# Recurrence readout with statistics in the token domain, a hand-over normalised tile by tile, and an experts' loop written out

## The chip, the cores and the metric

The kernel runs on one core of one Trainium2 chip. The metric is device time in microseconds (us) of one execution. Every time below comes from the runs of the kernel before or from its one profiled execution.

## The reference, cut to what matters

The program computes one forward pass in float32: two hybrid attention layers over 528 tokens (512 and 16 meta tokens), a final RMS norm, and then a second model over the 512 tokens and 256 context tokens: neighbourhood attention, a mixture of experts, an RWKV-7 recurrence in both directions, and a second mixture of experts. Three places are touched.

```python
# end of the first model, whose result is the second model's x
return rms_norm(h, final_g)[:, N_META:]

# readout of the recurrence; y is (token, head, 64)
mu = jnp.mean(y, axis=-1, keepdims=True)
var = jnp.mean(jnp.square(y - mu), axis=-1, keepdims=True)
yn = ((y - mu) * lax.rsqrt(var + RW_GN_EPS)).reshape(B, T, -1) * ln_g + ln_b
bonus = jnp.sum(jnp.sum(r[None] * kt * r_k, axis=-1, keepdims=True), axis=0) * v
return ((yn + bonus.reshape(B, T, -1)) * g) @ w_o
```

The mixture of experts has 16 experts with a 1024-wide hidden layer. Each takes 64 latent tokens and, in the first mixture, 32 context tokens too; its three weight matrices are 12 MiB.

## The kernel before, in words

The program is a row of stages. Each stage (`stage`, L48) is a block with one instruction stream per engine and ends with a barrier of all engines, so a stage takes as long as its slowest engine. Weights come through a ring of three slots of 2 MB (`load_chunk`, L73), which SyncE (its queue is called SP) fills when the stage's TensorE work has freed a slot.

**Hand-over** (`second_start`, L1064). It stands between the two models. SP issues `gain` (L1074), 17 small resident tensors (L2939), four rows of gates broadcast to 128 partitions (L1077), waits until the gates have landed (L1078), and only then issues the two tiles of context tokens (L1080). ScalarE sums the squares of four tiles (L1090) and takes one root over all four (L1093). VectorE inverts it (L1100), waits for `gain`, scales the four tiles (L1103), works on the modulation columns (L1108, L1113) and, last, waits for everything loaded (L1116). The first stages after it are `norm_turn` and `neighbour_project`, whose SP waits for TensorE's products before it loads a chunk.

**Experts** (`experts`, L1643), once after each attention layer. TensorE, ScalarE and VectorE each run a hardware loop of four passes (`Fori`) over a body of four experts. For each expert TensorE multiplies six half-matrix chunks (helper at L1750: 24 matmuls per chunk with context tokens, 8 without), places one-hot rows (L1760), turns the hidden rows (L1773) and the next expert's tokens (L1766). SP's and GpSimd's streams are already written out.

**Readout** (`rwkv_readout`, L2728). Y and V lie with 64 tokens times two heads on the partitions, and eight chunks of (pair, 64 features) behind each other. TensorE turns Y and V of one pair of heads at a time into features on partitions, with 16 matmuls against a 64-wide identity (L2764). It subtracts the mean by a product with a centring matrix (L2780), makes the gate (L2781), and sums the squares over each head by a product with ones (L2789). ScalarE copies (L2804), squares (L2813), adds the bias (L2817) and takes the root (L2821) of 128x512 tiles. VectorE inverts the 128x512 root (L2828) and does three more passes (L2830, L2833, L2836). GpSimd multiplies V by the bonus (L2755). The eight pairs follow each other with two buffers of each kind. After the stage, `hold` (L2839) issues the loads of the output weights, and `add_projection` (L999, matmuls at L1021) multiplies by them.

## Time and profile before

| | us |
|---|---|
| median of 3 runs | 3743.45 (3739.27 to 3749.13) |
| the profiled execution | 3760.89 |
| its span in the trace | 3759.1 |
| TensorE matmul busy | 3249.7 (86%) |
| VectorE busy | 1548.5 (41%) |
| ScalarE busy | 825.0 (22%) |
| GpSimd busy | 263.6 (7%) |
| mean granted clock of TensorE, share of full | 0.934 |

The profiled execution is one run with its own disturbances; 1.8 us lie outside its span. Matmul busy time is modelled from issue to end, and since matmuls are pipelined a busy TensorE says little by itself. What ends a wait is read from the name behind the arrow. A float32 matmul is recorded as two.

### The profile page before, as it was taken

How to read it: one execution, taken by the hardware profiler on the slowest of the kernel's cores; microseconds unless marked ns; L12 is line 12 of the kernel's file. 1: busy time of each engine (PE TensorE's matmuls, PEld its weight loads, DVE VectorE, ACT ScalarE, POOL GpSimd, SP SyncE). 2: the span in 40 equal slices, each digit the busy share in tenths (PEclk: the TensorE clock that was granted, in tenths of full speed). 3: DMA queues.
4: the chain of work that ended last, by engine and by line, in shares of the span. 5: the costliest groups of instructions: out<-in, count | busy, mean ns of one | idle time of the engine just before them, and what ended most of it. 6: DMA issues, size and time to landing. Idle time of an engine off the chain costs nothing. (4 is left out here: it accounts for less than half of the span.)

```text
span 3759.1 us, 73325 instructions
## 1 busy us (share of the span) xinstructions
PE 3249.7 (86%) x32052; PEld 1860.4 (49%) x32052; DVE 1548.5 (41%) x3486; ACT 825.0 (22%) x1777; POOL 263.6 (7%) x253
## 2 busy tenths in 40 slices
PE   7997999989699999699999969977888877677877
PEld 5845558555344564343343434557777753222222
DVE  4665435654212572422121244157777763311111
ACT  2104210142111570000000010046555530000000
POOL 0000000000000110000000000001222210000000
PEclk9998899988899999799999989979999998799999
DMA  6663046700221102599999921100000003699998
GB/s 176 170 184 108 23 96 165 210 24 29 86 67 48 32 25 90 216 379 337 345 367 338 347 67 67 40 25 4 4 4 4 4 30 122 254 401 399 403 400 347
DMA packets 147234, 605.36 MB, mean 161 GB/s; under 512 B 17264, under 2 KB 20144, under 8 KB 129904
## 3 DMA queue, kind: packets, MB, share of 16 engines
q1 hardware_dynamic: 140592, 579.19, 42.5%
q0 software_dynamic: 6336, 21.63, 2.5%
q8 instruction: 249, 4.08, 0.5%
q14 instruction: 57, 0.47, 0.0%
HBM read 576.00 MB, written 31.07 MB: 161 GB/s over the span
## 5 line engine op out<-in xcount | busy, mean ns | idle before, releaser
L1750 PE MATMUL psum<-ring,big 128*64 128x512 f32 (+1 forms) x6144 | 918.3, 506 | 117.9 <-DMA ring<-moe_w 99.8
L1750 PEld LDWEIGHTS psum<-ring,big 128*64 128x64 f32 (+1 forms) x6144 | 305.3, 126 | 711.0 <-issue 492.3
L1888 DVE TENSOR_TENSOR big<-big,psum 128x512 f32<-128x512 f32 (+1 forms) x48 | 27.3, 596 | 650.8 <-PE psum L1750 650.8
L391 PE MATMUL psum<-h_uT,ring 128*128 128x264 f32 x1280 | 290.5, 387 | 0.0
L520 DVE SCALAR_TENSOR_TENSOR h_O<-h_O,cond_silu 128x512 f32<-128x512 f32 x336 | 226.7, 744 | 102.7 <-DMA h_O<-ada_w 102.7
L391 PEld LDWEIGHTS psum<-h_uT,ring 128*128 128x128 f32 x1280 | 242.0, 190 | 46.5 <-issue 5.8
L1235 PE MATMUL psum<-ring,big 128*128 128x512 f32 x576 | 252.4, 598 | 1.7 <-PEq L55 1.7
L2328 PE MATMUL psum<-ring,gates 64*64 64x128 f32 (+1 forms) x5120 | 170.6, 257 | 81.8 <-ACT ring L2511 74.6
L2328 PEld LDWEIGHTS psum<-ring,gates 64*64 64x64 f32 x5120 | 134.3, 135 | 97.5 <-DVE ring L2669 83.5
L1900 DVE SCALAR_TENSOR_TENSOR big<-psum,big,gates 64x512 f32<-64x512 f32 (+1 forms) x128 | 78.8, 615 | 247.2 <-PE psum L1750 245.8
L1235 PEld LDWEIGHTS psum<-ring,big 128*128 128x128 f32 x576 | 109.5, 192 | 135.4 <-issue 135.4
L411 PE MATMUL psum<-ring,h_uT 128*128 128x512 f32 x384 | 170.0, 600 | 0.0
L1827 ACT ACTIVATE big<-psum 128x512 f32<-128x512 f32 (+1 forms) x48 | 23.5, 524 | 594.8 <-PE psum L1750 594.8
L1021 PE MATMUL psum<-ring,big 128*128 128x512 f32 x320 | 139.6, 598 | 16.6 <-DMA ring<-rw_w_o 15.5
L2669 DVE TENSOR_TENSOR ring<-ring,psum 64x256 f32<-64x256 f32 x288 | 120.9, 420 | 3.9
L411 PEld LDWEIGHTS psum<-ring,h_uT 128*128 128x128 f32 x384 | 72.6, 192 | 91.2 <-issue 91.1
L2511 ACT ACTIVATE gates<-psum 128x512 f32<-128x512 f32 x120 | 71.4, 595 | 183.7 <-PE psum L2328 183.5
L2056 PE MATMUL psum<-big,ring 128*128 128x512 f32 (+1 forms) x336 | 110.4, 491 | 0.0
L1718 POOL DMA_INDIRECT big<-rows,index x34 | 40.4, 1188 | 964.4 <-DVE big L1852 964.4
L1021 PEld LDWEIGHTS psum<-ring,big 128*128 128x128 f32 x320 | 61.3, 192 | 94.3 <-issue 78.0
L2328 PE MATMUL psum<-big,ring 64*64 64x64 f32 (+1 forms) x2816 | 105.5, 240 | 0.0
L1295 DVE TENSOR_REDUCE stat<-sq 128x8 f32<-128x512 f32 x24 | 16.5, 686 | 211.5 <-ACT sq L1274 211.5
(344 smaller groups left out, 4534.7 us busy)
## 6 DMA issues: line engine op xcount, KB each, us to landing
ring<-moe_w SPq DMA_DIRECT2D x192, 2048.0 KB, 10.6
h_O<-ada_w SPq DMA_DIRECT2D x192, 256.0 KB, 3.0
ring<-w_in SPq DMA_DIRECT2D x16, 2048.0 KB, 15.2
ring<-na_w_qkv SPq DMA_DIRECT2D x6, 2048.0 KB, 8.0
ring<-w_out SPq DMA_DIRECT2D x4, 2048.0 KB, 8.7
bias_rows<-na_table SPq DMA_DIRECT2D x16, 480.0 KB, 16.1
ring<-bias_rows SPq DMA_DIRECT2D x16, 360.0 KB, 3.0
rows<-big SPq DMA_DIRECT2D x10, 512.0 KB, 4.4
```

Source lines behind the costliest of these rows:

```text
L391: last = nc.tensor.matmul(bank(k, pair_bank(q) + h, NH), w[:, a, f * P:(f + 1) * P], uT[:, a, halves[h]], start=a == 0, stop=a == KD - 1)
L411: last = nc.tensor.matmul(bank(k, b), uT[:, a, t * P:(t + 1) * P], w[:, a, :], **st)
L520: nc.vector.scalar_tensor_tensor(into, ada(u), by, into, ALU.mult, ALU.add).then_inc(s.acc, 1)
L1021: last = nc.tensor.matmul(bank(k, j % BANKS)[0:rows, :], srcT[:, a, t * P:t * P + rows], w[:, a, :], start=a == 0, stop=a == KD - 1)
L1235: last = nc.tensor.matmul(bank(k, j % FIRST_BANKS), hT[:, a, t * P:(t + 1) * P], w[:, a, :], start=a == 0, stop=a == KD - 1)
L1718: nc.gpsimd.indirect_dma_start(xg[0:M, e % 2, :], None, k.rows[:, :], bass.IndirectOffsetOnAxis(ap=index[0:M, e % ROUND:e % ROUND + 1], ax ...
L1750: last = nc.tensor.matmul(bank(k, b, r.width)[q * r.n:(q + 1) * r.n, :], rowsT[:, half * HALF_K + n, r.first:r.first + r.n], w[:, n, q * r ...
L1900: last = nc.vector.scalar_tensor_tensor(y[r.first:r.first + r.n, x % 2, cols], bank(k, r.downs, r.width)[mine, :], gate[mine, x, 2 * r.at ...
L2056: last = nc.tensor.matmul(bank(k, j % BANKS, n), w[:, a, at:at + P], xs[m][:, a, first:first + n], **st)
L2328: last = nc.tensor.matmul(bank(k, b, width, at + p % QUAD * width)[to:to + CH, :], lhs(lo, p), rhs(lo, p), start=start and n == 0, stop=st ...
L2511: copy = lambda out, got: nc.scalar.activation(out, got, ACT.Copy)
L2669: last = tt(new[there], old[here], got[there, 1, :, :], ALU.add)
```

## The change

Three parts, each in a stage of its own.

1. In `second_start` the context tiles are issued before the resident tensors, and the gates move into the SP stream of `neighbour_project`, whose end now waits for them. ScalarE takes a root after each tile, VectorE does the modulation columns first, and then inverts and scales tile by tile.
2. In `experts` TensorE's loop is a Python loop: the four passes are written out, with constants for the registers. The loops of ScalarE and VectorE stay.
3. `rwkv_readout` is written anew. Mean, centring and variance are taken on Y before it is turned: VectorE reduces each chunk over 64 features (mean), centres it with a broadcast, reduces ScalarE's squares, and inverts 128x8 roots; GpSimd multiplies by the inverse. Meanwhile TensorE turns V and makes the gates of all pairs, with four banks for each, and ScalarE moves both to SBUF. When all eight chunks are normalised, TensorE turns Y pair by pair, VectorE adds the scaled Y to the V term, and the last product with the gate alternates between GpSimd (even pairs) and VectorE (odd pairs).

```diff
@@ second_start
         def _(sp):
             if norm:
                 sp.dma_start(gain[:, :], k.d["final_g"].partition_broadcast(P)).then_inc(s.gain_here, 16)
-            total = load_resident(k, sp, tiles, s.here)
-            for g in range(4):
-                sp.dma_start(k.gates[:, g, :], k.mod_rows[0, g % 2, (2, 5)[g // 2] * D:((2, 5)[g // 2] + 1) * D].partition_broadcast(P)).then_inc(k.gates_here, 16)
-            sp.wait_ge(k.gates_here, 64)
             for t in range(CT):
                 sp.dma_start(k.X[:, LT + t, :], k.d["ctx_2"][0, t * P:(t + 1) * P, :]).then_inc(s.here, 16)
+            total = load_resident(k, sp, tiles, s.here)
             sp.wait_ge(s.here, total + 16 * CT)
...
+            for t in range(LT if norm else 0):
+                dve.wait_ge(s.rooted, t + 1)
+                nc.vector.reciprocal(stat[:, 2, t:t + 1], stat[:, 1, t:t + 1]).then_inc(s.inverted, 1)
+                dve.wait_ge(s.inverted, t + 1)
+                if t == 0:
+                    dve.wait_ge(s.gain_here, 16)
+                nc.vector.scalar_tensor_tensor(k.X[:, t, :], k.X[:, t, :], stat[:, 2, t:t + 1], gain[:, :],
+                                               ALU.mult, ALU.mult).then_inc(s.normed, 1)
             dve.wait_ge(s.here, 16 * (len(tiles) + CT))
@@ neighbour_project, SP
+            for g in range(4):
+                sp.dma_start(k.gates[:, g, :], k.mod_rows[0, g % 2, (2, 5)[g // 2] * D:((2, 5)[g // 2] + 1) * D].partition_broadcast(P)).then_inc(k.gates_here, 16)
             for n in range(4):
                 sp.wait_ge(s.product, n_tiles * (n + 1))
...
             sp.wait_ge(s.between, 32)
+            sp.wait_ge(k.gates_here, 64)
@@ experts, TensorE
-            with pe.Fori(0, EXPERTS // ROUND) as it:
+            for it in range(EXPERTS // ROUND):
@@ rwkv_readout, GpSimd
+            def scale(c):
+                pool.wait_ge(s.inverted, c + 1)
+                nc.gpsimd.tensor_tensor(Y[:, c, :, :], Y[:, c, :, :], over(2, c), ALU.mult).then_inc(s.normed, 1)
+
+            pool.wait_ge(s.sorted, 4)
+            for p in range(QUAD):
+                shade(p)
+            for p in range(QUAD, PAIRS):
+                scale(p - QUAD)
+                shade(p)
+            for c in range(PAIRS - QUAD, n_chunk):
+                scale(c)
+            for p in range(0, PAIRS, 2):
+                pool.wait_ge(s.closed, p + 1)
+                nc.gpsimd.tensor_tensor(mixT[:, p, :], term(p), gate(p), ALU.mult)
@@ rwkv_readout, TensorE
             for p in range(PAIRS):
...
                 pe.wait_ge(s.shaded, p + 1)
+                if p >= QUAD:
+                    pe.wait_ge(s.v_out, p - QUAD + 1)
+                turned(V, p % QUAD, p, p >= QUAD).then_inc(s.v_turned, 1)
...
+            pe.wait_ge(s.normed, n_chunk)
+            for p in range(PAIRS):
+                if p < QUAD:
+                    pe.wait_ge(s.v_out, p + QUAD + 1)
+                else:
+                    pe.wait_ge(s.gate_out, p + 1)
+                turned(Y, p, p, False).then_inc(s.y_turned, 1)
@@ rwkv_readout, ScalarE
+            for n in range(n_chunk):
+                act.wait_ge(s.centred, n + 1)
+                if n >= 2:
+                    act.wait_ge(s.spread, n - 1)
+                nc.scalar.activation(square(n), Y[:, n, :, :], ACT.Square).then_inc(s.squared, 1)
+                if n:
+                    root(n - 1)
+                act.wait_ge(s.v_turned, n + 1)
+                nc.scalar.activation(term(n), bank(k, n % QUAD), ACT.Identity, bias=k.ln_cols[:, 1, n:n + 1]).then_inc(s.v_out, 1)
+                act.wait_ge(s.gate_made, n + 1)
+                nc.scalar.activation(gate(n), bank(k, QUAD + n % QUAD), ACT.Copy).then_inc(s.gate_out, 1)
+            root(n_chunk - 1)
@@ rwkv_readout, VectorE
+            def mean(c):
+                nc.vector.tensor_reduce(stat[:, 0, c, :], Y[:, c, :, :], AX.X, ALU.add).then_inc(s.summed, 1)
+                dve.wait_ge(s.summed, c + 1)
+                nc.vector.scalar_tensor_tensor(Y[:, c, :, :], over(0, c), -1.0 / CH, Y[:, c, :, :], ALU.mult, ALU.add).then_inc(s.centred, 1)
...
+            for c in range(n_chunk):
+                mean(c)
+                if c >= 2:
+                    invert(c - 2)
+                if c >= 1:
+                    spread(c - 1)
...
             for p in range(PAIRS):
...
+                dve.wait_ge(s.y_turned, p + 1)
                 dve.wait_ge(s.v_out, p + 1)
+                nc.vector.scalar_tensor_tensor(term(p), bank(k, p), k.ln_cols[:, 0, p:p + 1], term(p), ALU.mult, ALU.add).then_inc(s.closed, 1)
+                if p % 2:
+                    dve.wait_ge(s.closed, p + 1)
+                    dve.wait_ge(s.gate_out, p + 1)
+                    nc.vector.tensor_tensor(mixT[:, p, :], term(p), gate(p), ALU.mult)
```

VectorE in the readout. Before, each pair of heads has these four full-width passes:

```order
L2825 SCALAR_TENSOR_TENSOR big<-head_ones_sb,ident_sb 128x128
L2828 RECIPROCAL big<-big 128x512
L2830 TENSOR_TENSOR big<-psum,big 128x512
L2833 SCALAR_TENSOR_TENSOR big<-big,ln_cols_sb 128x512
L2836 TENSOR_TENSOR big<-big,psum 128x512
```

Now each chunk has two reductions, one centring pass and a reciprocal of 128x8, and the pairs come at the end:

```order
L2840 TENSOR_REDUCE big<-big 128x8
L2834 TENSOR_REDUCE big<-big 128x8
L2836 SCALAR_TENSOR_TENSOR big<-big 128x512
L2844 RECIPROCAL big<-big 128x8
...
L2858 SCALAR_TENSOR_TENSOR big<-psum,ln_cols_sb,big 128x512 x2
L2862 TENSOR_TENSOR big<-big 128x512
```

The reciprocal went from 512 columns to 8, and the statistics of all chunks now stand ahead of the first turned Y.

TensorE at the end of the first mixture's loop body, before (L1750 the products, L1785 the loop):

```order
L1766 MATMUL psum<-ident_sb,big 128x96 x8
L1750 MATMUL psum<-ring,big 64x512 x8
L1750 MATMUL psum<-ring,big 32x256 x16
L1743 REGISTER_ALU
L1750 MATMUL psum<-ring,big 64x512 x8
L1750 MATMUL psum<-ring,big 32x256 x16
L1785 REGISTER_ALU
L1785 COMPARE_AND_BRANCH
```

Now, between any two experts:

```order
L1760 MATMUL psum<-big 128x2 x6
L1773 MATMUL psum<-ident_sb,big 128x128 x6
L1766 MATMUL psum<-ident_sb,big 128x96 x8
L1750 MATMUL psum<-ring,big 64x512 x8
L1750 MATMUL psum<-ring,big 32x256 x16
```

The branch is gone after every fourth expert; the matmuls are the same.

SP's queue at the hand-over, before (end of the stage) and now (its beginning, then its end with the next SP stage):

```order
L2939 DMA head_ones_sb<-head_ones 128x128
L1077 DMA gates<-mod_rows 128x1024 x4
L1080 DMA X<-ctx 128x1024 [waits gates_here]
L1080 DMA X<-ctx 128x1024
```

```order
L1075 DMA gain<-final_g 128x1024
L1077 DMA X<-ctx 128x1024 x2
L2966 DMA na_q_cols_sb<-na_q_cols 128x1
...
L2966 DMA head_ones_sb<-head_ones 128x128
L52 UNCONDITIONAL_BRANCH [waits here_1]
L1196 UNCONDITIONAL_BRANCH [waits barrier_Pool_Activation_PE_DVE_SP_release]
L1199 DMA gates<-mod_rows 128x1024 x4
```

The wait on the gates is gone from between the two groups of loads, and the gates stand behind the barrier.

## Rows read from the trace of the kernel before

**Rows 1.** Waits between 950 and 1000 us: waiter, releaser, total, times, longest.

```profile
SPq L1080 <- DMA gates<-mod_rows: 7.5, 1, 7.5
...
DVE na_q_cols_sb L1116 <- DMA X<-ctx: 9.0, 1, 9.0
```

**Rows 2.** Timeline of the hand-over: start, duration, engine, line, operation.

```profile
958.59 0.34 SPq L1074 DMA_DIRECT2D gain<-final_g  x1
...
966.49 5.25 DVE L1103 SCALAR_TENSOR_TENSOR X<-X,stat,gain 128x1024 f32<-128x1024 f32 x4 [2.74 <-DMA gain<-final_g]
...
981.60 0.15 DVE L1116 TENSOR_SCALAR na_q_cols_sb<-na_q_cols_sb 128x1 f32<-128x1 f32 x1 [9.00 <-DMA X<-ctx]
```

**Rows 3.** Timeline of TensorE in the first mixture of experts.

```profile
1615.62 32.76 PE L1750 MATMUL psum<-ring,big 128*64 128x512 f32 x288
...
1651.62 32.76 PE L1750 MATMUL psum<-ring,big 128*64 128x512 f32 x288
...
1702.69 23.56 PE L1750 MATMUL psum<-ring,big 128*64 128x512 f32 x192 [4.01 <-issue]
...
1802.31 34.46 PE L1750 MATMUL psum<-ring,big 128*64 128x512 f32 x288
...
1856.40 23.56 PE L1750 MATMUL psum<-ring,big 128*64 128x512 f32 x192 [3.69 <-issue]
...
2007.78 23.28 PE L1750 MATMUL psum<-ring,big 128*64 128x512 f32 x192 [5.42 <-issue]
```

**Rows 4.** Windows: length, busy PE, PEld, DVE, ACT, POOL; PEclk, DMA share, GB/s.

```profile
1590.00:1700.00 110.00, 108.39 (x954) 44.88 (x946) 25.93 (x68) 5.23 (x12) 7.97 (x6) 1.00 0.98 373
...
3300.00:3400.00 100.00, 78.39 (x358) 27.37 (x356) 13.96 (x33) 4.87 (x7) 8.05 (x6) 0.96 1.02 400
...
1699.00:1707.00 8.00, 4.31 (x12) 1.35 (x14) 3.18 (x6) 0.00 (x0) 1.43 (x1) 0.79 0.98 337
...
3055.00:3062.00 7.00, 5.08 (x66) 4.32 (x67) 0.29 (x1) 2.11 (x6) 5.87 (x6) 0.51 0.86 335
```

**Rows 5.** Timeline of TensorE in the second mixture, fourth and fifth expert.

```profile
3329.29 3.65 PE L1750 MATMUL psum<-ring,big 128*64 128x512 f32 x16 [2.77 <-DMA ring<-moe_w]
...
3361.91 9.09 PE L1750 MATMUL psum<-ring,big 128*64 128x512 f32 x32 [2.92 <-DMA ring<-moe_w]
```

**Rows 6.** Timeline of the readout and the projection after it.

```profile
3055.09 1.94 PE L2764 MATMUL psum<-eye_sb,big 64*64 64x64 f32 x32 [3.00 <-PEq L55]
...
3063.26 1.15 PE L2764 MATMUL psum<-eye_sb,big 64*64 64x64 f32 x32
...
3110.47 0.69 DVE L2836 TENSOR_TENSOR big<-big,psum 128x512 f32<-128x512 f32 x1
...
3119.91 56.93 PE L1021 MATMUL psum<-ring,big 128*128 128x512 f32 x128 [15.52 <-DMA ring<-rw_w_o]
```

**Rows 7.** Groups of the readout, 3054 to 3118 us: count, busy, mean ns, idle before.

```profile
L2828 DVE RECIPROCAL big<-big 128x512 f32<-128x512 f32 x8 | 26.8, 3346 | 11.7 <-ACT big L2821 11.7
...
L2755 POOL TENSOR_TENSOR big<-big,rw_bonus 128x512 f32<-128x512 f32 x8 | 8.2, 1058 | 2.1 <-ACT rw_bonus L2797 2.1
L2833 DVE SCALAR_TENSOR_TENSOR big<-big,ln_cols_sb 128x512 f32<-128x512 f32 x8 | 6.0, 752 | 0.3
...
L2804 ACT ACTIVATE big<-psum 128x512 f32<-128x512 f32 x8 | 4.8, 597 | 6.7 <-PE psum L2764 6.7
...
L2821 ACT ACT_TABLE_LOAD x1 | 1.3, 1283 | 0.0
```

**Rows 8.** Groups elsewhere with like operations; the last is one line's min, median, max.

```profile
L1295 DVE TENSOR_REDUCE stat<-sq 128x8 f32<-128x512 f32 x11 | 7.5, 686 | 56.6 <-ACT sq L1274 56.6
...
L1298 DVE RECIPROCAL stat<-stat 128x8 f32<-128x8 f32 x11 | 2.2, 203 | 3.0 <-ACT stat L1276 3.0
...
L2300 POOL TENSOR_TENSOR X<-ring,rw_R 128x512 f32<-128x512 f32 x16 | 28.2, 1765 | 72.8 <-DVE ring L2606 72.8
...
L2606 DVE SCALAR_TENSOR_TENSOR ring<-ring,big x24: 681/693/1012, 2496.4 to 2993.7; 128x512 f32<-128x512 f32 x24
```

More of the change, by code:

```diff
@@ L1066, in second_start @@
     nc = k.nc
-    with ExitStack() as mem, stage(k, "here scaled summed rooted step gain_here biased") as (block, s):
+    with ExitStack() as mem, stage(k, "here scaled summed rooted inverted normed gain_here biased") as (block, s):
         sb = lambda n, shape: mem.enter_context(nc.sbuf_tensor(f"{n}{k.stage_no}", shape, F32))
@@ L2725, in _, with rwkv_readout @@
             in_turn(slot)
-def rwkv_readout(k, Y, V, sums, tg, mixT, spare, g2):
+def rwkv_readout(k, Y, V, sums, tg, mixT, g2, stat, rest):
     nc = k.nc
@@ L2735, in rwkv_readout @@
     sums, bonus = sums
-    buf = lambda n: lambda p: spare[:, (2 * n + p % 2) * SEQ:(2 * n + p % 2 + 1) * SEQ]
-    yT, squares, root, term, scaled = (buf(n) for n in range(5))
-    centre = spare[:, 10 * SEQ:10 * SEQ + P]
-    Y_AT, MIDDLE_AT, GATE_AT = (lambda p: p % 2), (lambda p: 2 + p % 2), (lambda p: 4 + p % 2)
-    V_AT, SPREAD_AT = 6, 7
-    with stage(k, "g2_here restored sorted shaded centred y_turned v_turned middle gate_made spread "
-                  "y_out squared v_out rooted inverted normed shifted gated") as (block, s):
+    cut = lambda t, n: t[:, n * SEQ:(n + 1) * SEQ]
+    terms, low, high, squares = rest
+    term = lambda p: cut(terms, p)
+    gate = lambda p: cut(low if p < QUAD else high, p % QUAD)
+    square = lambda c: cut(squares, c % 2).rearrange("p (a i) -> p a i", i=CH)
+    stat = stat[:, 0:3 * n_chunk * PAIRS].rearrange("p (n c a) -> p n c a", n=3, c=n_chunk)
+    over = lambda n, c: stat[:, n, c, :].unsqueeze(2).to_broadcast([P, PAIRS, CH])
+    with stage(k, "g2_here restored sorted shaded v_turned v_out gate_made gate_out "
+                  "summed centred squared spread rooted inverted normed y_turned closed") as (block, s):
         @block.sync
@@ L2798, in _, with root @@
                                          ACT.Copy).then_inc(s.sorted, 1)
[L2800 to L2821 removed]
+            def root(c):
+                act.wait_ge(s.spread, c + 1)
+                nc.scalar.activation(stat[:, 1, c, :], stat[:, 1, c, :], ACT.Sqrt, bias=64e-5, scale=1.0 / CH).then_inc(s.rooted, 1)
@@ new lines, in spread, with invert @@
+            def spread(c):
+                dve.wait_ge(s.squared, c + 1)
+                nc.vector.tensor_reduce(stat[:, 1, c, :], square(c), AX.X, ALU.add).then_inc(s.spread, 1)
+            def invert(c):
+                dve.wait_ge(s.rooted, c + 1)
+                nc.vector.reciprocal(stat[:, 2, c, :], stat[:, 1, c, :]).then_inc(s.inverted, 1)
+            for c in range(n_chunk):
[4 more added lines that the diff above has]
+                    spread(c - 1)
@@ L2879, in rwkv_layer @@
         mixT = flat(A)[:, 0:KD * SEQ].rearrange("p (a b) -> p a b", a=KD)
-        rwkv_readout(k, Y, V, (sums, bonus), tg, mixT, flat(E), flat(A)[:, KD * SEQ:KD * SEQ + D])
+        rest = [flat(E)[:, 0:KD * SEQ], flat(C)[:, KD * SEQ:], left, flat(E)[:, KD * SEQ:KD * SEQ + D]]
+        rwkv_readout(k, Y, V, (sums, bonus), tg, mixT, flat(A)[:, KD * SEQ:KD * SEQ + D], flat(A)[:, KD * SEQ + D:], rest)
     hold(k)
```

76 lines of the change are left out of this document (12 added, 64 removed).

## The prediction

> **What bounds the kernel now.** Every stage ends at a barrier, so I read each of the three touched stages by itself, in the timeline and the waits. A microsecond taken off the last engine of a stage is taken off the whole time, unless the stage behind it is held by something that runs across the barrier.
>
> *Hand-over.* VectorE's last instruction starts at 981.60 [rows 2], after 9.0 us of waiting for the context tiles; those were issued after SP had waited 7.5 us for the gates, which nobody in this stage reads [rows 1]. VectorE's scaling had ended at 971.7 (966.49 + 5.25), with a few small operations behind it; those passes had waited for `gain` until 966.49 [rows 2]. A loading order bounds this stage.
>
> *First mixture of experts.* TensorE runs an expert without a gap: two begin at 1615.62 and 1651.62, 36.0 us apart, of which 32.76 are the products of six chunks [rows 3]. At the three loop ends it stands still for 4.01, 3.69 and 5.42 us, released by "issue", that is by nothing but its own sequencer [rows 3]. The four chunks behind each stop take 23.56, 23.56 and 23.28 us, where four sixths of 32.76 are 21.84. So the stage is bound by TensorE and its instruction stream. The weight stream is near it: 373 GB/s in a stretch without stops, where the second mixture shows that 400 can be had [rows 4].
>
> *Second mixture.* It is bound by that stream: DMA share 1.02 [rows 4], and TensorE waits for weights at the start of an expert whether a loop end lies before it (2.92 us) or not (2.77) [rows 5]. The two starts are 32.6 us apart, 12.6 MB at 386 GB/s.
>
> *Readout.* It runs from 3055.09 to 3111.16, 56.1 us [rows 6]. VectorE waits 11.7 us for the first root and is then busy to the end; of a pair's 5.5 us the full-width reciprocal is 3.35 [rows 7].
>
> **The change, part by part.**
>
> *Hand-over.* The gates (four issues) and the wait for them leave the stage. The context tiles are issued right behind `gain`. `gain` lands where it did, at about 966.4, and 1 MB behind it at 400 GB/s [rows 4] takes 2.6 us: 969. Two more issues put the last small load at about 968 and its landing at 970 to 971, est. VectorE then decides: from 966.5 four times 1.31 (5.25 / 4) [rows 2], a reciprocal of 0.2 at most [rows 8] and 0.05 of hand-off, 6.2: it ends at 972.9 instead of 981.75. The per-tile roots are ready before (`gain` is what is late) and cost nothing. **-8.8**; bounds -5.5 (small loads landing as late as the gates did) and -9.5. The gates now go out at the start of the projection stage, ahead of SP's waits for products: SP is free there, the ring is full, the queue empty; cost 0. Without that cover it would be the 7.5 us of rows 1.
>
> *Experts' loop written out.* First mixture: the three stops go, 4.01 + 3.69 + 5.42 = 13.1. Behind a stop the granted clock is at its lower level for a while (mean 0.79 of full over 8 us around the first, [rows 4]; the levels are 1.2 and 2.4 GHz), which made the four chunks 1.72, 1.72 and 1.44 longer, 4.9 in all. But the same loss of 1.7 shows in experts with no stop (34.46 against 32.76, [rows 3]), six times by my count of this trace, so it may come anyway. Some wait for weights may come too, since each stop let the loads catch up. I take **-16**: all stops and about half of the rest. Bounds 0 and -19. The register additions go too; they are too small to price. What new stall can the written-out stream bring? The loop body of four experts is already straight code of its kind, and in the 110 us up to about the first stop TensorE is busy 108.39 [rows 4]; I price the rest at 0. ScalarE's and VectorE's loops keep their branches; both have two or more chunks (11 us) before they are wanted. Second mixture: **0**, by rows 5.
>
> *Readout.* Removed: the centring and ones products, 8 x 3.35 of reciprocal, and the two buffers that tied TensorE, ScalarE and VectorE in one circle. Added, from like operations: per chunk two reductions at 0.69, a reciprocal of 128x8 at 0.20 [rows 8], a centring pass at 0.72 (between 0.69 and 0.75, [rows 7, 8]); on GpSimd one product at 1.05 [rows 7]. The path, in five pieces:
> - To the first inverse, 9.4 est: the bonus copies 1.0 and GpSimd's first product 1.05 with a wait of 0.4 before it, V turned 1.94 at the lower clock (granted clock 0.51 here, 1.2 GHz) [rows 4, 6], the gate product about as much, 1.7, two ScalarE passes at 0.60, the table load and root 1.5 [rows 7], the inverse 0.2, and 0.4 of hand-offs. Behind ScalarE's in-order waits for V and gate, VectorE's own 5 us of work is hidden.
> - Four periods with GpSimd's two products in each. GpSimd is slowed by VectorE when both read two SBUF tensors: 1765 ns for L2300, which starts 0.07 us after such a VectorE operation, against 1058 for one beside an idle VectorE; and once VectorE's L2606 took 1012 instead of 693 [rows 7, 8]. So I let them exclude each other. Inverse 0.20, GpSimd 1.05 + 1.05, centring 0.72, hand-offs 0.1: 3.1 x 4 = 12.5. Alone, VectorE's period would be 0.20 + 0.69 + 0.69 + 0.72 + 0.1 = 2.4, so the exclusion costs 2.8 here, and about 1.1 in the last piece.
> - The last chunks, with one GpSimd product that falls beside reductions: 5.5 (2.4, 1.3, 1.8).
> - The last product on GpSimd 1.1.
> - Y turned: two pairs at 1.94 (TensorE has been idle some 4 us), six at about 1.05 back to back, hand-offs 0.1 each, 10.3; the last closing pass and gate product behind it, with VectorE and GpSimd excluding each other, 3.0.
>
> Sum 41.8 against 56.1: **-14.5** rounded (the pieces overlap a little). Bounds: 36 if nothing excludes and TensorE is never slow, 48 if TensorE turns everything at 1.94; -20 and -8.
>
> Here a rule bears on the choice. The Trainium skill, SBUF — State Buffer, "Who interferes with whom", says that a VectorE instruction with two SBUF inputs and a GpSimd instruction that reads SBUF take an exclusive lock, and that a VectorE instruction with one SBUF input does not contend. By that rule the readout takes 41.8, with the waits placed as above; without it 37.9. The trace agrees for GpSimd (1765 against 1058 ns) and shows VectorE held up once (1012 against 693).
>
> *Behind the readout.* TensorE waits 8.75 us after the end of the readout for output weights that are only issued then [rows 6]; that distance stays. The routing and the second mixture start earlier by the whole gain, since their loads are tied to slots and stages and not to a clock.
>
> Sum: -8.8 - 16 - 14.5 = **-39.3**. The profiled execution of 3760.89 would become 3721.6. It is 0.5% above the median, and nothing in the terms scales with that, so the forecast is 3743.45 - 39.3 = 3704, rounded.
>
> **The rivals.**
>
> 1. *The weights take the stops back.* The first mixture becomes bound by its stream, and each stop returns as waits for `ring<-moe_w`. For it: 373 GB/s and a share of 0.98 [rows 4]. Against it: 108.39 of 110 us busy at 373 GB/s, and 400 GB/s elsewhere [rows 4]. Gain 8.8 + 14.5 = 23: 3720.
> 2. *No exclusion in the readout.* The centring pass and GpSimd run side by side, 2.8 + 1.1 = 3.9 less: 3700. For it: VectorE's median at L2606 is undisturbed; against it: the 1765 and 1012 ns [rows 8].
> 3. *A slow readout.* ScalarE's in-order waits and a cold TensorE keep it at about 50 us; gain 6 there: 3712.
> 4. *A starved TensorE stream, slower than before.* Straight code is fetched once instead of looped; if the fetch fell behind the saturated weight queues once per expert at the price of a loop end (4.4 us, mean of rows 3), the first mixture alone would pay 16 x 4.4 = 70 and save 13: -8.8 - 14.5 + 57 = +34, 3777. It decides from eight such stops on. Against it: the first pass through the body had none.
> 5. *It does little.* The stops come back, the small loads land late, and the readout gains 5: gain 10, 3733.
>
> **How the numbers follow.** Forecast 0.60, rival 1 0.12, rival 2 0.10, rival 3 0.11, rival 4 0.03, rival 5 0.04. What can be told from no change is about 0.3%, 11 us: faster 0.93, same 0.04, slower 0.03. Range: the low end takes nearly all favourable bounds (-9.5 - 19 - 20 = -48.5) and a few us of spread between runs, 3690; the high end takes in rivals 1 and 3 and reaches about half way from rival 1 to rival 5, 3726.
>
> **What would show it.** Hand-over: no wait of SP for the gates, VectorE's last operation 6 to 7 us after `gain` lands, next stage about 9 us earlier. First mixture: no "issue" stop of 3 us or more on L1750, an expert every 36.0 to 37.7 us, stage shorter by 13 to 19. Second mixture: 32.6 us per expert as before. Readout: 38 to 46 us, some GpSimd products well over 1.05 us, Y turned in about 10 us. I am wrong if waits for `ring<-moe_w` appear in the first mixture with more than 5 us in total, if stops of "issue" stay, or if the readout stays over 48.

## The result and the profile after

| us | before | after |
|---|---|---|
| median of 4 runs each | 3741.36 (3732.58 to 3749.13) | 3696.53 (3688.93 to 3703.95) |
| the profiled execution | 3760.89 | 3688.93 |
| its span | 3759.1 | 3687.2 |
| mean granted clock of TensorE | 0.934 | 0.943 |

The ratio of after to before is 0.9877, with an interval of [0.9858, 0.9895]: about 46 us less (the medians are 44.8 apart), where 39.3 were forecast (against the forecast's own base that is a ratio of 0.9895). All ratios here and below compare executions in the faster state of the chip; one execution of e9 (3760.34 us, granted clock 0.901) was in the slower one and is left out. The two profiled executions are 72 us apart. So some 26 us of what the two traces show is no work of the change, and the first task is to separate them. The stages are cut at the same events in every kernel:

| stage (us) | before | after | difference |
|---|---|---|---|
| start to issue of `gain` (untouched) | 958.6 | 947.5 | -11.1 |
| hand-over: to the first turning of the next stage (L118) | 27.3 | 18.4 | -8.9 |
| to the first expert product (untouched) | 566.3 | 561.4 | -4.9 |
| first mixture, first to last L1750 | 607.9 | 578.4 | -29.5 |
| to the readout (untouched) | 894.9 | 891.2 | -3.7 |
| readout, to the issue of the output weights | 56.9 | 39.0 | -17.9 |
| to the second mixture (untouched) | 121.3 | 121.3 | 0.0 |
| second mixture | 517.2 | 521.4 | +4.2 |

The untouched stretches give 19.7 of the 72. The same code took between 947.5 and 963.1 us up to the issue of `gain` in the twelve profiled executions of this study, so that part is spread between executions. The 4.9 us ahead of the first expert product are not so plainly spread: that stretch took 566.3 to 566.6 us in the four kernels that keep the loop of four experts in the first mixture (before, e1, e3, e5) and 561.3 to 564.7 in the other eight. Most of it lies in the first 20 us behind the hand-over, where the granted clock rises later (over the ten us from 10 us on it is 0.66 before and 1.00 after). In e1 and e10 the code up to there is the same, and yet one took 566.3 us and the other 561.6; no run shows why. The page after has GpSimd busier (263.6 before) and all other engines less, TensorE by 46 us (3249.7 before):

```profile
PE 3203.8 (87%) x32020; PEld 1845.8 (50%) x32020; DVE 1534.7 (42%) x3500; ACT 820.9 (22%) x1780; POOL 277.9 (8%) x265
...
L1750 PE MATMUL psum<-ring,big 128*64 128x512 f32 (+1 forms) x6144 | 906.9, 502 | 106.1 <-DMA ring<-moe_w 53.7
```

**Hand-over.** The timeline after, as [rows 2] (start, duration, engine, line, operation, and in brackets the idle time before it and its releaser):

```profile
947.47 0.34 SPq L1075 DMA_DIRECT2D gain<-final_g  x1
...
947.86 0.96 SPq L1077 DMA_DIRECT2D X<-ctx  x2
...
952.68 1.14 SPq L2966 DMA_DIRECT2D ln_cols_sb<-ln_cols  x1
...
955.44 1.28 DVE L1110 SCALAR_TENSOR_TENSOR X<-X,stat,gain 128x1024 f32<-128x1024 f32 x1 [6.37 <-DMA gain<-final_g]
...
958.25 0.43 SPq L2966 DMA_DIRECT2D head_ones_sb<-head_ones  x1
959.63 1.28 DVE L1110 SCALAR_TENSOR_TENSOR X<-X,stat,gain 128x1024 f32<-128x1024 f32 x1
961.51 0.15 DVE L1113 TENSOR_SCALAR na_q_cols_sb<-na_q_cols_sb 128x1 f32<-128x1 f32 x1 [0.60 <-DMA head_ones_sb<-head_ones]
```

`gain` lands 8.0 us after its issue, about as before (958.59 to 966.49, [rows 2]). Behind it VectorE scales tile by tile, 1.40 us from one to the next, and its last instruction starts 6.1 us after the first scaling. Before it was 15.1 us (966.49 to 981.60). The wait of 9.00 us for the context tiles has become one of 0.60 for the last of the small loads: the two ends of this stage now meet almost exactly. The small loads are issued in 0.43 us each, but three of them took 0.80 to 1.14; by my estimate from these rows (1.6 us more than three issues of 0.43) the last wait would be gone without that.

**First mixture.** TensorE after, as [rows 3]:

```profile
1590.50 32.76 PE L1750 MATMUL psum<-ring,big 128*64 128x512 f32 x288
...
1626.50 32.76 PE L1750 MATMUL psum<-ring,big 128*64 128x512 f32 x288
...
1770.39 27.31 PE L1750 MATMUL psum<-ring,big 128*64 128x512 f32 x240
1798.04 5.52 PE L1750 MATMUL psum<-ring,big 128*64 128x512 f32 x48 [0.34 <-DMA ring<-moe_w]
...
2058.59 32.76 PE L1750 MATMUL psum<-ring,big 128*64 128x512 f32 x288
...
2094.59 10.97 PE L1750 MATMUL psum<-ring,big 128*64 128x512 f32 x96
```

An expert still takes 36.0 us. No stop of "issue" as long as half a microsecond is left in the stage, and the waits for weights come to 0.34 us in all. This execution also has none of the losses of 1.7 us that were counted six times before, which is luck, as the experiments show.

**Second mixture.** TensorE after, as [rows 5], and the window beside [rows 4] (length, busy PE, PEld, DVE, ACT, POOL, granted clock, DMA share, GB/s):

```profile
3253.49 9.82 PE L1750 MATMUL psum<-ring,big 128*64 128x512 f32 x32 [3.38 <-issue]
...
3286.45 5.28 PE L1750 MATMUL psum<-ring,big 128*64 128x512 f32 x16 [3.31 <-issue]
```

```profile
3280.00:3380.00 100.00, 81.77 (x356) 29.11 (x354) 13.93 (x33) 3.58 (x6) 8.01 (x6) 0.91 1.01 397
```

The wait at an expert's start now says "issue", 48.1 us in 15 times over the stage, where before it named the weights. Read alone this looks like rival 4, a starved instruction stream. It stands at the same place and is about as long as before (2.77 and 2.92, [rows 5]). Over the stage L1750 waited 101.5 us in all, "issue" and weights together, where before it waited 99.2 for weights alone, and the weight stream is as full: share 1.01, 397 GB/s. With the loop written out the label changed and the wait did not; the next section tests that.

**Readout.** VectorE after, from its first to its last operation, which answers to [rows 6, 7]:

```profile
2996.82 0.69 DVE L2834 TENSOR_REDUCE big<-big 128x8 f32<-128x512 f32 x1 [2.22 <-PEq L55]
...
3005.88 0.20 DVE L2844 RECIPROCAL big<-big 128x8 f32<-128x8 f32 x1 [3.71 <-ACT big L2815]
3006.00 0.63 DVE L2840 TENSOR_REDUCE big<-big 128x8 f32<-128x512 f32 x1
3006.55 0.68 DVE L2834 TENSOR_REDUCE big<-big 128x8 f32<-128x512 f32 x1
3007.26 1.51 DVE L2836 SCALAR_TENSOR_TENSOR big<-big 128x512 f32<-128x512 f32 x1
3008.70 0.19 DVE L2844 RECIPROCAL big<-big 128x8 f32<-128x8 f32 x1
...
3018.46 0.69 DVE L2836 SCALAR_TENSOR_TENSOR big<-big 128x512 f32<-128x512 f32 x1
...
3021.26 0.20 DVE L2844 RECIPROCAL big<-big 128x8 f32<-128x8 f32 x1 [0.41 <-ACT big L2815]
...
3033.80 1.20 DVE L2862 TENSOR_TENSOR big<-big 128x512 f32<-128x512 f32 x1
```

GpSimd in the same stretch:

```profile
3006.17 1.04 POOL L2761 TENSOR_TENSOR big<-big 128x512 f32<-128x512 f32 x1 [3.07 <-DVE big L2844]
3007.17 1.06 POOL L2757 TENSOR_TENSOR big<-big,rw_bonus 128x512 f32<-128x512 f32 x1
```

And TensorE, which turns Y and then waits for the output weights as before:

```profile
3022.63 9.23 PE L2782 MATMUL psum<-eye_sb,big 64*64 64x64 f32 x256 [3.75 <-POOL big L2761]
3043.78 2.93 PE L1021 MATMUL psum<-ring,big 128*128 128x512 f32 x3 [11.91 <-DMA ring<-rw_w_o]
```

The stage is 38.2 us (2996.82 to 3035.00), before 56.1. One period shows what sets it. The centring pass starts at 3007.26, when GpSimd's product of V by the bonus has run for 0.09 us. It ends at 3008.77: 0.5 us behind GpSimd's end at 3008.23, after 1.51 us in place of 0.69. The periods between inverses are 2.82, 2.80, 2.80 and 2.79 us with these two products in each, and 1.98 in the one behind them, where GpSimd has none on V left and the centring at 3018.46 takes 0.69.

### The profile page after: what moved, and what is told of

Its sections match the earlier page's. It is cut to its first block and busy times, and to the rows that moved or that the text cites. A ratio compares the mean times of both kernels' runs of the same rounds, so it can differ in the third digit from the quotient of the medians.

```text
span 3687.2 us, 73003 instructions
## 1 busy us (share of the span) xinstructions
PE 3203.8 (87%) x32020; PEld 1845.8 (50%) x32020; DVE 1534.7 (42%) x3500; ACT 820.9 (22%) x1780; POOL 277.9 (8%) x265
## 5 line engine op out<-in xcount | busy, mean ns | idle before, releaser
L1750 PE MATMUL psum<-ring,big 128*64 128x512 f32 (+1 forms) x6144 | 906.9, 502 | 106.1 <-DMA ring<-moe_w 53.7
L1750 PEld LDWEIGHTS psum<-ring,big 128*64 128x64 f32 (+1 forms) x6144 | 305.6, 126 | 687.2 <-issue 524.2
L1888 DVE TENSOR_TENSOR big<-big,psum 128x512 f32<-128x512 f32 (+1 forms) x48 | 27.3, 597 | 637.2 <-PE psum L1750 637.2
L1827 ACT ACTIVATE big<-psum 128x512 f32<-128x512 f32 (+1 forms) x48 | 23.5, 524 | 596.0 <-PE psum L1750 595.9
L1833 ACT ACTIVATE big<-psum 128x512 f32<-128x512 f32 (+1 forms) x48 | 23.5, 524 | 359.2 <-PE psum L1773 359.2
## 6 DMA issues: line engine op xcount, KB each, us to landing
ring<-moe_w SPq DMA_DIRECT2D x192, 2048.0 KB, 10.3
bias_rows<-na_table SPq DMA_DIRECT2D x16, 480.0 KB, 15.6
```

The lines of the kernel that those rows point to most:

```text
L1750: last = nc.tensor.matmul(bank(k, b, r.width)[q * r.n:(q + 1) * r.n, :], rowsT[:, half * HALF_K + n, r.first:r.first + r.n], w[:, n, q * r ...
```

## The experiments

Each row of stages comes from one profiled execution. Those with several executions have a ratio too, to the kernel before on the same chip. "First" and "second" are the two mixtures, "stops" the waits of "issue" over 3 us on L1750 in the first.

| kernel | time, ratio to before | hand-over | first | stops | readout | second |
|---|---|---|---|---|---|---|
| before (its profile) | 3741.36 | 27.3 | 607.9 | 4.01, 3.69, 5.42 | 56.9 | 517.2 |
| after | 3696.53, 0.9877 | 18.4 | 578.4 | none | 39.0 | 521.4 |
| e1 hand-over alone | 3734.29, 0.9972 [0.9958, 0.9986] | 18.4 | 603.8 | 4.05, 3.97, 4.48 | 58.3 | 517.5 |
| e2 loop alone | 3725.42, 0.9945 [0.9925, 0.9966] | 26.6 | 581.5 | none | 58.2 | 518.2 |
| e3 readout alone | 3727.23, 0.9953 [0.9937, 0.9970] | 27.1 | 597.0 | 4.04, 3.96, 3.95 | 38.9 | 522.4 |
| e4 second mixture looped | 3699.80, 0.9885 [0.9864, 0.9907] | 18.3 | 580.3 | none | 38.9 | 519.1 |
| e5 only the second written out | 3755.39, one run | 27.7 | 597.7 | 3.84, 3.93, 3.97 | 56.8 | 520.7 |
| e6 loops over two experts | 3704.28, 0.9894 [0.9877, 0.9911] | 18.4 | 589.5 | none | 39.6 | 519.4 |
| e7 V products first | 3698.60, 0.9873 [0.9851, 0.9895] | 18.5 | 580.2 | none | 35.6 | 520.7 |
| e8 writes only | 3703.15, one run | 18.5 | 583.7 | none | 37.0 | 519.0 |
| e9 weights early | 3689.76, 0.9838 [0.9815, 0.9861] | 18.4 | 585.0 | none | see below | 521.1 |
| e10 changed, again | 3705.48, 0.9892 [0.9870, 0.9914] | 18.1 | 586.2 | none | 39.7 | 520.2 |

### The three parts apart

**e1**: the kernel before with the new hand-over.

```diff
 # second_start, neighbour_project: as in the change
 # experts, rwkv_readout: as before
```

> The kernel before with only the hand-over changed (context tiles before the resident tensors, gates moved behind the barrier, tile-by-tile normalisation). My account: the stage from the issue of gain to the first transposition of the next stage takes 18.4 us as in the changed kernel, against 27.3 before, and the whole is 9 us (0.24%) faster. Rival, that the moved gate loads cost something in the projection stage: the hand-over is 9 us shorter but the stages from there to the first mixture's first product are longer than 566 us.

The hand-over took 18.4 us and -0.28% is 10.5 us. Nothing behind it slipped: the next stage found its gates in time (to the first mixture 566.3 us, as before). The whole stage's gain is a gain of the program.

**e2**: the kernel before with the experts' loop of TensorE written out.

```diff
-            with pe.Fori(0, EXPERTS // ROUND) as it:
+            for it in range(EXPERTS // ROUND):
```

> The kernel before with only TensorE's experts' loop written out, in both mixtures. Theory A (stops, and the clock losses behind them): the first mixture, from its first product to its last, loses 13.1 + 4.9 = 18 us and keeps some 34 us experts with a lowered clock, so about 590 against 608. Theory B (the stops also bring on the later clock losses, so these go too): 578 as in the changed kernel. Both: the second mixture takes 520.8 instead of 516.6 if its 4 us are caused by the written-out stream, 516.6 if they were chance. Whole: 14 (A) to 25 (B) us faster.

No stop was left, and the first mixture took 581.5 us: between the two theories, for a reason that follows below.

**e3**: the kernel before with the new readout.

```diff
 # rwkv_readout and its call in rwkv_layer: as in the change
 # second_start, neighbour_project, experts: as before
```

> The kernel before with only the readout changed. My account: the stage takes 38.2 us against 56.1, everything else as before, 18 us (0.48%) faster. The first mixture keeps its three stops of 3.7 to 5.4 us; if its clock losses are chance, their number differs from the six counted in the kernel before, and if they follow from the stops it is similar.

The readout alone takes 38.9 us, as within the change, against 56.9. The three gains measured alone add up to 0.28 + 0.55 + 0.47 = 1.30% against 1.23% for the change at once (intervals of 0.14 to 0.21 on each): the parts are independent, as stages cut by barriers should be.

The first mixture needs more care, since a part of what it lost before was not the loop's. In e3 the loop has all of its stops (timeline of TensorE, first mixture):

```profile
1700.53 23.56 PE L1750 MATMUL psum<-ring,big 128*64 128x512 f32 x192 [4.04 <-issue]
...
1850.46 23.56 PE L1750 MATMUL psum<-ring,big 128*64 128x512 f32 x192 [3.96 <-issue]
...
2000.94 23.56 PE L1750 MATMUL psum<-ring,big 128*64 128x512 f32 x192 [3.95 <-issue]
```

and the four chunks behind each stop are 1.72 us over the 21.84 that they take at the full clock, as before. But the stage took 597.0 us and not 607.9. Most of the difference is in losses away from any stop: six chunks in a row in 34.46 us instead of 32.76. The trace of before has six of them (9.7 us), e1 three (5.1), e3 none and e5 two (3.4); with the loop written out the changed kernel has none, e2 two (3.3), e4 one (1.7), e7 none, e8 three (5.0), e9 four (6.7) and e10 four (6.8). So they come with and without stops, and to identical code: none in the changed kernel, four in e10. One of e10, the last small matmuls before it and the windows of both:

```profile
1707.44 1.10 PE L1766 MATMUL psum<-ident_sb,big 96*128 96x96 f32 x8
```

```profile
1705.20:1708.40 3.20, 3.14 (x30) 2.90 (x26) 2.50 (x8) 0.87 (x2) 0.84 (x1) 1.00 1.12 452
1708.40:1715.70 7.30, 7.30 (x52) 2.49 (x52) 2.31 (x8) 0.00 (x0) 0.36 (x1) 0.77 0.69 267
```

The granted clock is 0.77 of full in the chunk that is longer. Their place is not random: all 31 in the twelve traces begin at an expert's fifth chunk, right behind the 3.3 us of small matmuls (L1760, L1773, L1766), and only in the fifth to the ninth and the thirteenth to the sixteenth expert. TensorE does not stand still there, and most experts pass the same place without a loss; what decides stays open.

What the loop costs is the stops (12.3 us on average over the four kernels that have them) and 4.6 behind them, 16.9 in all: eleven of the twelve stops have a longer chunk right behind, the third of e5 has not. The means of the stage agree: 601.6 in four kernels with the loop, 582.2 in seven without, 19.4 apart, of which 2.5 are left for chance. Of the 29.5 between the two first traces, some 12.6 were therefore luck on one side and bad luck on the other.

### What the label "issue" means in the second mixture

**e4**: the changed kernel, with a loop again in the second mixture.

```diff
-            for it in range(EXPERTS // ROUND):
...
+            def passes(it, size):
...
+            written_out, size = (True, 4) if with_ctx else (False, 4)
+            if written_out:
+                for it in range(EXPERTS // size):
+                    passes(it, size)
+            else:
+                with pe.Fori(0, EXPERTS // size) as it:
+                    passes(it, size)
```

> The changed kernel with the loop of four passes kept in the second mixture alone. Theory F (the written-out stream has to be fetched through saturated DMA queues, where the loop body of the second mixture stayed in TensorE's instruction memory): the second mixture takes 516.6 us as before, 4 pages of instructions are fetched in it instead of 14, no stops at its loop ends, and the whole is 4 us faster than the changed kernel. Rival C (the 4 us are chance, or come from the changed time at which the stage starts): 520 to 521 us again.

**e5**: the kernel before, with only the second mixture written out.

```diff
-            with pe.Fori(0, EXPERTS // ROUND) as it:
...
+            def passes(it, size):
...
+            written_out, size = (False, 4) if with_ctx else (True, 4)
```

> The kernel before with TensorE's loop written out in the second mixture alone. The looped second mixture took 517.2 and 517.5 us with the old readout (before, e1) and 522.4 and 519.1 with the new one (e3, e4); written out it took 521.4 with the new and 518.2 with the old. If the readout ahead of it sets the difference, this run (old readout, written out) takes 517 to 518; if the written-out stream sets it, 520 to 522. 14 or 15 pages of instructions are fetched in it in either case. First mixture as before, with three stops of about 4 us.

In e4 the waits name the weights again (TensorE, second mixture):

```profile
3264.67 8.91 PE L1750 MATMUL psum<-ring,big 128*64 128x512 f32 x32 [3.13 <-DMA ring<-moe_w]
...
3297.07 3.65 PE L1750 MATMUL psum<-ring,big 128*64 128x512 f32 x16 [2.88 <-DMA ring<-moe_w]
```

and they are as long: 103.8 us over the stage. The stage: with the loop 517.2, 517.5, 522.4, 519.1 and 519.4 (mean 519.1), written out 521.4, 518.2, 520.7, 520.7, 519.0, 521.1 and 520.2 (mean 520.2). A microsecond at most is between them, less than the spread within either. Neither theory's number came in e4 (516.6, or 520 to 521; measured 519.1). The +4.2 of the first pair of traces is therefore not shown to be the written-out code's. It is not clearly the new readout's either: the mean is 518.4 in the four kernels with the old readout and 520.4 in the eight with the new one, but e5, with the old one, took 520.7 where 517 to 518 were expected if the readout decides. What makes this stage vary from 517 to 522 stays open.

### Why the loop stopped in one mixture and not in the other

**e6**: the changed kernel with a loop in both mixtures again, over a body of two experts.

```diff
-            for it in range(EXPERTS // ROUND):
-                for x in range(ROUND):
-                    e = it * ROUND + x
+            def passes(it, size):
+                for x in range(size):
+                    e = it * size + x
...
+            written_out, size = (False, 2) if with_ctx else (False, 2)
...
+                with pe.Fori(0, EXPERTS // size) as it:
+                    passes(it, size)
```

> The changed kernel with TensorE's loop kept in both mixtures, but with a body of two experts and eight passes. Theory M (a stop at a loop end is the re-fetch of a body that is too large to stay in TensorE's instruction memory; two experts of the first mixture are half of it): no stops of 3 us or more in the first mixture, few pages fetched in it (39 when written out, 46 with the body of four), first mixture 578 to 582 us, total as the changed kernel. Theory J (each taken branch costs about 4 us whatever the body): seven stops, 28 us of them and some 12 us of lowered clock behind them, first mixture about 618 us, total 38 us slower than the changed kernel.

Seven loop ends, none of them a stop. One lies in the first of these two experts of the first mixture, behind its second chunk; the second expert has none, and they take the same time:

```profile
1600.80 32.76 PE L1750 MATMUL psum<-ring,big 128*64 128x512 f32 x288
...
1636.89 32.76 PE L1750 MATMUL psum<-ring,big 128*64 128x512 f32 x288
```

The DMA view of that stage in e6 (queue and kind, packets, MB, share of 16 engines):

```profile
q8 instruction: 5, 0.08, 0.1%
```

and of the same stage in the changed kernel:

```profile
q8 instruction: 39, 0.64, 0.4%
```

Before, with a body of four, it was 46. For one expert with context tokens the trace has 314 products and 314 weight loads, 628 instructions (the turning matmuls, L1766 and L1773, are recorded once and not twice). The straight code of 16 experts, 10048, came in 39 packets, some 258 to a packet. A body of four is 2512 and was fetched anew in every pass (46 packets for four passes, more than the 39 of the straight code); a body of two is 1256, five packets at that rate, and five were fetched for all eight passes. In the second mixture, where an expert has 232, a body of four is 928 and four packets were fetched in all. So the stop is the price of a body that TensorE's instruction store does not hold, not of a branch. The Trainium skill, Runtime: NRT & Kernel Launch, "Instruction fetch mechanics", gives that store as 2048 instructions for TensorE and says that a taken branch to a page that is not held forces a fetch before anything goes on. The trace agrees as far as it goes: 2512 stops, 1256 and 928 do not, and no run here shows where between 1256 and 2512 the limit lies. The same section counts only a window of two pages of 256 instructions as held; by that 1256 and 928 would have to stop too, and the trace does not agree.

e6 also puts the losses of 1.7 us in their place. It has no stop and hardly any fetch traffic, and lost 9.8 us in six of them. With experts 36.09 us apart instead of 36.00, 1.4 in all, that is why its stage took 589.5 us and not the 578 to 582 that were expected. An expert of e6 with one:

```profile
2002.62 34.46 PE L1750 MATMUL psum<-ring,big 128*64 128x512 f32 x288
```

### What holds VectorE in the readout

**e7**: the changed kernel; GpSimd makes all eight products on V first, and then the eight on Y.

```diff
-            for p in range(QUAD):
+            for p in range(PAIRS):
                 shade(p)
-            for p in range(QUAD, PAIRS):
-                scale(p - QUAD)
-                shade(p)
-            for c in range(PAIRS - QUAD, n_chunk):
+            for c in range(n_chunk):
                 scale(c)
```

> The changed kernel with GpSimd's eight bonus products ahead of all its products with the inverse. Theory X (GpSimd's products and VectorE's centring exclude each other, which makes the centring 1.51 us in five periods): the centring falls to 0.69 to 0.75 us from the fourth chunk on, the period from 2.80 to about 2.3, the readout from 39.0 to about 37 us (from its first load to the load of the output weights). Theory S (ScalarE's in-order waits set the period): the period stays at 2.8. In the total 2 us are below what can be told.

VectorE in e7, two periods with nothing of GpSimd's beside the centring pass:

```profile
3025.74 0.69 DVE L2833 SCALAR_TENSOR_TENSOR big<-big 128x512 f32<-128x512 f32 x1
3026.35 0.20 DVE L2841 RECIPROCAL big<-big 128x8 f32<-128x8 f32 x1
...
3027.73 0.69 DVE L2833 SCALAR_TENSOR_TENSOR big<-big 128x512 f32<-128x512 f32 x1
3028.34 0.19 DVE L2841 RECIPROCAL big<-big 128x8 f32<-128x8 f32 x1
```

The period is 1.99 us instead of 2.80 (one of the four, in which a product does fall beside the pass, has 2.46) and the stage 35.6 instead of 39.0, 3.4 less. Of these, 2.4 lie between the first and the last inverse (13.0 us instead of 15.4). Most of the rest is in turning Y, which ran at the full clock in e7 (7.68 us at a granted clock of 1.00) and not in the changed kernel (9.23 at 0.82). And e7 took two things from the four periods: the collision, and a product of 1.06 us from GpSimd. A period without the product might be short for that reason.

**e8** tells them apart: GpSimd keeps two instructions of about half a microsecond in that place, which write the tile and read nothing; this leaves out the bonus term of half the heads.

```diff
             for p in range(QUAD, PAIRS):
                 scale(p - QUAD)
-                shade(p)
+                v = V[:, 0:n_chunk, p, :]
+                nc.gpsimd.memset(v, 0.0).then_inc(s.wiped, 1)
+                pool.wait_ge(s.wiped, p - QUAD + 1)
+                nc.gpsimd.memset(v, 0.0).then_inc(s.shaded, 1)
```

> The changed kernel with GpSimd's last four bonus products replaced by two fills with zero each, of the same size and at the same place in its order; this leaves out the bonus term of half the heads. Theory X with the exclusion tied to what GpSimd reads: GpSimd is as busy beside the centring, but the centring takes 0.69 us instead of 1.51, and the period falls to about 2.3 us. Theory Y (any GpSimd work beside VectorE slows it): the centring stays above 1 us.

GpSimd in e8:

```profile
3026.99 0.53 POOL L2769 MEMSET big<- 128x512 f32 x1
3027.58 0.53 POOL L2771 MEMSET big<- 128x512 f32 x1
```

and VectorE in the same microsecond:

```profile
3027.11 0.69 DVE L2839 SCALAR_TENSOR_TENSOR big<-big 128x512 f32<-128x512 f32 x1
3027.72 0.20 DVE L2847 RECIPROCAL big<-big 128x8 f32<-128x8 f32 x1
```

GpSimd is busy under all but 0.06 us of the centring pass, and the pass takes 0.69 us. The first four periods are 1.98 to 2.00, and from the first to the last inverse it is 13.0 us as in e7; the stage, 37.0, turned Y with two pairs at the lower clock. So it is reading, not being busy, that excludes the two; writing does not. The Trainium skill, SBUF — State Buffer, "Who interferes with whom", says just this of a GpSimd instruction that only writes SBUF, and the trace agrees (0.69 us beside a writer, 1.51 beside a reader). The reductions, with one input in SBUF, took 0.63 and 0.68 us beside GpSimd's reading products at 3006.00 and 3006.55 above, as much as alone.

### What the readout now waits for, and a faster version

After the end of the readout, TensorE still waits 8.8 us for output weights that are issued only then (3035.00 to 3043.78; forecast: 8.75, [rows 6]). **e9** is e7 with these weights issued in the readout itself.

```diff
 # rwkv_readout, SP's stream, behind the load of x_saved
+            for c in range(k.c, k.c + 3):
+                if c + SLOTS < len(k.chunks):
+                    load_chunk(k, sp, c + SLOTS)
...
-    hold(k)
+    k.c += 3
```

> The kernel of e7 with the loads of the output weights and of the first expert chunk issued in the readout's own SP stream, so that the stage that only issued them goes. TensorE's start of the output projection stood 8.75 us behind the end of the readout in the kernel before, waiting for weights issued after it. If no ring slot is in use in the readout and the weights were the only thing waited for: the distance falls to 1 us or less, and the whole is 8 us faster than e7, about 3687 to 3690 us (ratio to the kernel before 0.985). Rival: 6 MB of loads beside the 2 MB restore of X delay the gate matrix (512 KB, issued ahead of them) and the readout becomes longer by up to 5 us.

VectorE's last operation of the readout in e9:

```profile
3053.76 1.20 DVE L2862 TENSOR_TENSOR big<-big 128x512 f32<-128x512 f32 x1
```

and TensorE's first product of the projection:

```profile
3055.78 6.57 PE L1021 MATMUL psum<-ring,big 128*128 128x512 f32 x11 [4.42 <-PEq L55]
```

The gap is 0.8 us (3054.96 to 3055.78), and only the barrier is in it. The readout itself, from VectorE's first to its last operation, takes 36.0 us where e7's took 34.7 and e10's 38.9; Y was turned in 9.1 us at partly the lower clock instead of 7.68, so the rival, loads that delay the gate matrix, is not needed for that. From the loads at the start of the readout to the first expert product of the second mixture it is 150.2 us in e9, and 161.0 in e10: 10.8 less.

**e10** is the changed kernel once more, on the chip of e9.

> The changed kernel once more, unedited, beside e9 on the same chip. Ratio to the kernel before 0.986 to 0.990. First mixture 578 to 584 us without a stop of the sequencer; second mixture between 517 and 522 us, since looped and written-out runs have both shown values at either end.

It gave 0.9892 [0.9870, 0.9914], the first result again. Against it e9 is 15.7 us faster by the medians (3689.76 against 3705.48), where the shorter readout (36.0 against 38.9) and the 8.0 taken off the gap make 10.9; the rest is within the spread of e9 (3680.62 to 3700.73). It is the best kernel of this study, at 0.9838 [0.9815, 0.9861] of before.

## Why the prediction held, and where its terms were off

The time is inside the range, 7.5 us below the forecast; the repeat, at 3705.48, is 1.5 above it. Point by point:

- **Hand-over, -8.8.** Measured -9.0 to its end (23.2 us from the issue of `gain` to VectorE's last operation before, 14.2 now). The pieces: scaling 5.5 us where 6.2 were forecast (with the inverses it is 1.40 a tile, not 1.31 + 0.25), and the last small load 0.60 later than the scaling instead of before it. These two errors nearly cancel, which is luck; both are within the bounds.
- **First mixture, -16.** What the loop cost is 16.9 by the four profiles that have it (12.3 + 4.6); the stages' means differ by 19.4. The step that failed is "all stops and about half of the rest": the clock loss behind a stop does not come anyway. In no kernel without the stops is the chunk at those three places longer. The other losses come in any number, and there the step was right to leave them out. That the trace of before had 9.7 us of them, and the trace after none, would have misled anyone who reads only the two.
- **No waits for weights in their place** (rival 1): held. At 357 to 365 GB/s over the whole stage the waits for weights stayed within 2 us in every kernel without a loop. Straight code did not starve (rival 4): held, and e4 shows that 48 us of "issue" in the second mixture are the old waits under another name. The second mixture at 0: held on the means, +1.1 us, within the spread.
- **Readout, -14.5.** Measured -17.9: the term that was most mis-sized. By its pieces, forecast and measured: first inverse 9.4 and 9.3; four periods 12.5 and 11.2; last chunks 5.5 and 4.2; last product 1.1 and 1.2; Y turned 10.3 and 9.2; tail 3.0 and 3.1. Three of six carry the 3.6.
  - The periods: the step was "inverse 0.20, GpSimd 1.05 + 1.05, centring 0.72". In the trace the centring is issued under the second product and ends 0.5 us after it, not 0.7 with a hand-off; a period is 2.80. That they exclude each other was right, and its price here was near: the four periods are 2.8 us shorter in e7 (8.4 instead of 11.2, with part of one collision left) and 3.3 shorter in e8 (8.0), where 2.8 were forecast; by the last inverse 2.4 of it remain in both. The further 1.1 that the forecast laid to it in the last piece no run tests.
  - The last chunks: VectorE's own period was put at 2.4 from like operations at 0.69 and hand-offs of 0.1. It is 1.99, for operations on one engine overlap by about 0.1 us each (3006.00 + 0.63 is later than 3006.55), and there is no hand-off to pay.
  - Y turned: the lower clock came, in part. Behind 3.75 us of idle time the first pair took 1.26 us, the second and third 1.92 and 1.81, and the other five followed 0.93 apart where 1.05 and a hand-off were put:

```profile
3023.80:3026.60 2.80, 2.80 (x58) 2.80 (x58) 1.67 (x3) 0.00 (x0) 1.27 (x1) 0.50 0.02 6
3026.60:3031.90 5.30, 5.26 (x174) 5.12 (x170) 4.93 (x7) 0.00 (x0) 2.54 (x2) 0.97 0.01 3
```

  The same code took 9.93 us in e10, where the first three pairs were all at the lower clock, and in e7, behind 2.14 us of idle time, 7.68. So some of the 1.1 us here is luck.
- **The distance to the output weights stays**: 8.75 before and 8.78 after. **The routing and what follows start earlier by the whole gain**: 121.3 us from the readout to the second mixture in both.
- **Rival 3** (a readout of some 50 us) and **rival 5** (little of it works) are out by the stages: 38.2 us, no stop, small loads in time. **Rival 2** (no exclusion) is excluded by e7 and e8, though its time for the readout, 37.9, is nearer to what was measured than the forecast's 41.8. A time that fits is no proof of a mechanism: the gain came from overlap elsewhere, and removing the exclusion took another 2.4.

What stays open: what decides whether a loss of 1.7 us comes, what moves the second mixture between 517 and 522 us, and why the stretch ahead of the first mixture is some 4 us longer in the four kernels with the loop of four experts.

## What to carry to other kernels

Take row statistics in the layout where they are narrow: the inverse of a 128x512 root cost 3.35 us [rows 7] and of a 128x8 root 0.20. Order loads by who in this stage waits for them, and issue the first weights of the next stage within this one; behind a barrier they cost their full flight (8.8 us here). Size a loop body on TensorE by its instructions (1256 ran free, 2512 paid about 5.6 us per pass), and keep GpSimd's reading operations away from VectorE's two-input ones, which can be done by order alone. Compare several profiles before a difference in a long TensorE stage is called an effect: identical code differed by 8 us in the first mixture, and by up to 15.6 in the stretch before the hand-over.

## What the runs showed of the hardware

- The same loop is free or not by the size of its body (e6), with packets of the instruction queue as the witness: 5 against 46.
- Losses of 1.7 us come in float32 products without any stop before them, none to six in 580 us, at a granted clock of 0.77; all 31 begin right behind the same 3.3 us of small matmuls.
- Written-out code turns the releaser of a wait from `ring<-moe_w` into "issue" at about the same length (15 of 2.8 to 3.6 us in the changed kernel; 101.5 us of waits over the stage, 99.2 before, 103.8 in e4).
- SP's issues of small loads, 0.43 us each, rose to between 0.80 and 1.14 for three in a row at the hand-over.
- A VectorE pass with two inputs in SBUF took 1.51 us when begun 0.09 us after a GpSimd product began, and 0.69 beside GpSimd's writes.
